# Chunked RWKV-7 and GLA scans: a chunk's tail issued inside the next chunk's inverse, and its small products cut to 64 columns

## The chip, the cores and the metric

The kernel runs on one core of a Trainium2 chip. The metric is device time in microseconds (us) of one execution; the kernel before takes 3583.4 us (median of 3 runs, 3581.79 to 3586.96). Engines are named as in the profile: PE is TensorE (matmul), PEld its weight loads, DVE VectorE, ACT ScalarE, POOL GpSimd, SP SyncE, which issues the DMAs.

## The reference: what is computed

One layer of a hybrid model on 2176 tokens (128 context, 2048 latent): a projection feeds three mixers (RG-LRU, RWKV-7, GLA), their outputs are projected back and added; then comes an expert-choice MoE. The change touches only the two matrix-state scans, each run forward and backward:

```python
# RWKV-7, 6 heads of 64, per token
sa = einsum('dbhij,dbhj->dbhi', S, -kk_t)
S  = S * w_t + sa[..., None] * (kk_t * a_t) + v_t[..., None] * k_t
o  = einsum('dbhij,dbhj->dbhi', S, r_t)
# GLA, 4 heads, keys 48, values 96, per chunk of 64 tokens
o = att @ v + (q * exp(b)) @ S
S = S * exp(b_last)[..., None] + (k * exp(b_last - b)).T @ v
```

## The kernel before, in words

The scans are one stage of the program, `stage_scans`, between the mixers' projection and the mixers' output. It takes 34 chunks of 64 tokens (`NCH`; 2 of context). The two directions are the two groups g = 0 and 1 and are worked on together. A group holds 3 tiles of 2 RWKV heads, one head in partitions 0 to 63 and one in 64 to 127 (`HALVES`), and 2 tiles of 2 GLA heads.

For RWKV a chunk needs the inverse of a triangular 64x64 matrix for each head. It is built by doubling, in five levels. A level l is `joined(c, l)` (PE: LM times T into the banks pY), `joined` on DVE (adds the identity, giving Ys), `grown(c, l)` (PE: Ys times U into the banks pYU), then `turned(c, l)` on DVE (transposes it into T) and `grown` on ACT (copies it to U). ACT's copy waits until DVE has transposed (`t_step`), except at level 5. A level's first product needs the T of the level before, so the levels are one chain through PE and DVE, and other products stand between them to cover it. These others are, in words: `values_seen` and `read_out` (keys against decayed keys and against reads, to KR and RK), `state_seen` (the state read by the chunk, to X), `keys_by_token` (BK, a transpose), `strict` (the next chunk's triangular matrix), `keys_turned`, and `attention` (GLA, 7 products for each tile and group).

What follows the inverse is here called the tail: `corrected` (U times X, written to SV), `state_grown` (the new RWKV state), `old_state_out` and `chunk_out` (the two parts of the output), `gla_added` and `gla_output` (the GLA state and output). The tail of chunk c has the banks pY, pYU and the free part of g1, and stands behind level 5 of chunk c; chunk c+1 begins when it is issued.

Each engine executes what it is given in order, and waits on semaphores; the order of each engine's work is written out by hand, in four functions `chunk(c)` (POOL, ACT, PE, DVE) and in SP's loop. So a wait holds up all that stands behind it on its engine. `SP` loads chunk c+3 after `freed(c)`, which waits for the states and outputs of chunk c, and then stores chunk c.

A product of `heads` is two matmuls, one for each half of the partitions, with 64 rows and 64 columns of the array each. `read_out` and `keys_by_token` use 64 rows and 128 columns, `state_grown` and `chunk_out` 128 rows and 64 columns. All are fp32, and the trace has two records for each such matmul: 12 matmuls of a level are 24 records.

## Time and profile before

| what | value |
|---|---|
| median of 3 runs | 3583.4 us |
| the profiled execution | 3593.6 us, its span 3591.9 us |
| PE busy in the span | 3171.3 us (88%) |
| DVE, ACT, POOL busy | 2275.4, 1611.8, 840.6 us |
| scans, first to last product | about 981 to 1825 us of the span |
| TensorE clock granted, mean of the span | 0.944 of full speed |

In a timeline row the first number is when the group of instructions starts, the second how long it lasts; x24 is the number of records; a bracket gives how long the engine was idle before it and what ended that. Records of PE overlap, and their ends are modelled: the time that a group really takes from the engine is the difference between its start and the next one's. A name such as scn_b is a PSUM bank with its number left out.

### The profile page before, as it was taken

The numbers are of one execution on the slowest core, as the hardware profiler recorded it, in microseconds if no ns is written. First come the engines' busy times: TensorE is split into PE (matmuls) and PEld (weight loads), VectorE is DVE, ScalarE is ACT, GpSimd is POOL, SyncE is SP. The second block draws the span as 40 slices with busy tenths as digits, with TensorE's granted clock in tenths as the row PEclk, the third lists the DMA queues.
The fourth block names the chain that finished last, engine by engine and source line by source line (L and its number), as shares of the span: only waits on it lengthen the run. The fifth ranks groups of instructions, "written<-read, shape, count | busy, mean of one in ns | idle before, by whom it ended". The sixth has DMA issues, their size and how long they took to land. (4 is left out here: it accounts for less than half of the span.)

```text
span 3591.9 us, 91692 instructions
## 1 busy us (share of the span) xinstructions
PE 3171.3 (88%) x37497; PEld 2899.1 (81%) x37497; DVE 2275.4 (63%) x4488; ACT 1611.8 (45%) x2909; POOL 840.6 (23%) x1189
## 2 busy tenths in 40 slices
PE   4899979999599999999959981799999999999992
PEld 1887867767499889999957760799999999999992
DVE  2575548995467777777768768455555555555553
ACT  1412756665444444444446640344444444444442
POOL 0200000000165655666622200111211111121000
PEclk7999989999799999999979985899999999999996
DMA  4464335665644544444356632556666655666646
GB/s 177 110 208 154 98 92 189 207 190 164 179 103 97 125 128 103 101 96 96 85 136 190 188 105 94 171 184 188 191 207 187 188 184 185 188 203 192 187 150 217
DMA packets 582979, 560.14 MB, mean 156 GB/s; under 512 B 211408, under 2 KB 527120, under 8 KB 581692
## 3 DMA queue, kind: packets, MB, share of 16 engines
q1 hardware_dynamic: 552496, 467.21, 43.8%
q0 software_dynamic: 30160, 88.35, 8.9%
q8 instruction: 236, 3.87, 0.5%
q14 instruction: 87, 0.71, 0.1%
HBM read 418.20 MB, written 137.23 MB: 155 GB/s over the span
## 5 line engine op out<-in xcount | busy, mean ns | idle before, releaser
L3253 DVE TENSOR_TENSOR exp_wlo<-exp_raw,exp_whi 128x2048 fp32r<-128x2048 f32 x192 | 439.9, 2292 | 361.8 <-ACT exp_whi L3208 354.2
L3208 ACT CAST exp_whi<-exp_raw 128x2048 fp32r<-128x2048 f32 x189 | 360.0, 1905 | 75.2 <-DMA exp_raw<-in_w_up 75.2
L986 PE MATMUL mix_acc<-proj_hThi,mix_wlo 128*128 128x448 f32 (+3 forms) x920 | 357.0, 388 | 14.0 <-DVE mix_wlo L1354 14.0
L986 PE MATMUL mix_acc<-proj_hTlo,mix_whi 128*128 128x448 f32 (+3 forms) x920 | 334.8, 364 | 0.0
L986 PE MATMUL mix_acc<-proj_hThi,mix_whi 128*128 128x448 f32 (+3 forms) x920 | 334.5, 364 | 0.0
L3137 PE MATMUL moe_o<-moe_hidhi,exp_wlo 128*128 128x272 f32 x1024 | 306.2, 299 | 0.0
L3137 PE MATMUL moe_g<-moe_xThi,exp_wlo 128*128 128x272 f32 x1024 | 299.7, 293 | 1.0 <-DVE moe_xTlo L3257 1.0
L3124 POOL DMA_INDIRECT y<-moe_yo,exp_sel x32 | 51.3, 1603 | 1051.3 <-DVE moe_yo L3267 1046.4
L3137 PE MATMUL moe_g<-moe_xThi,exp_whi 128*128 128x272 f32 x1024 | 296.9, 290 | 0.0
L3137 PE MATMUL moe_u<-moe_xThi,exp_wlo 128*128 128x272 f32 x1024 | 296.6, 290 | 0.0
L3137 PE MATMUL moe_o<-moe_hidhi,exp_whi 128*128 128x272 f32 x1024 | 296.6, 290 | 0.0
L3137 PE MATMUL moe_u<-moe_xThi,exp_whi 128*128 128x272 f32 x1024 | 296.4, 289 | 0.0
L3137 PE MATMUL moe_g<-moe_xTlo,exp_whi 128*128 128x272 f32 x1024 | 295.6, 289 | 0.0
L3137 PE MATMUL moe_u<-moe_xTlo,exp_whi 128*128 128x272 f32 x1024 | 295.0, 288 | 0.0
L3137 PE MATMUL moe_o<-moe_hidlo,exp_whi 128*128 128x272 f32 x1024 | 294.5, 288 | 0.0
L1941 ACT COPY scn_U<-scn_b 128x192 f32<-128x192 f32 x340 | 106.4, 318 | 280.1 <-DVE scn_T L2251 204.8
L957 POOL DMA_DIRECT2D proj<-mix_out x115 | 62.5, 544 | 715.7 <-ACT mix_out L1126 715.7
L986 PEld LDWEIGHTS mix_acc<-proj_hThi,mix_wlo 128*128 128x128 f32 (+1 forms) x920 | 172.2, 187 | 59.4 <-issue 42.5
L3137 PEld LDWEIGHTS moe_g<-moe_xThi,exp_wlo 128*128 128x128 f32 x1024 | 193.5, 189 | 2.0 <-DVE moe_xTlo L3257 1.4
L3137 PEld LDWEIGHTS moe_o<-moe_hidhi,exp_wlo 128*128 128x128 f32 x1024 | 192.9, 188 | 1.8
L3137 PEld LDWEIGHTS moe_g<-moe_xTlo,exp_whi 128*128 128x128 f32 x1024 | 193.8, 189 | 0.0
L3137 PEld LDWEIGHTS moe_g<-moe_xThi,exp_whi 128*128 128x128 f32 x1024 | 193.3, 189 | 0.0
(369 smaller groups left out, 8556.2 us busy)
## 6 DMA issues: line engine op xcount, KB each, us to landing
exp_raw<-in_w_gate SPq DMA_DIRECT2D x64, 1024.0 KB, 5.3
exp_raw<-in_w_up SPq DMA_DIRECT2D x64, 1024.0 KB, 5.2
exp_raw<-in_w_down SPq DMA_DIRECT2D x64, 1024.0 KB, 5.3
scn_plain<-rec SPq DMA_DIRECT2D x68, 384.0 KB, 3.6
rec<-mix_arena SPq DMA_DIRECT2D x24, 896.0 KB, 4.3
proj<-mix_out POOLq DMA_DIRECT2D x88, 224.0 KB, 2.3
scn_grc<-grec SPq DMA_DIRECT2D x136, 128.0 KB, 3.9
mix_arena<-in_w_ada SPq DMA_DIRECT2D x12, 1024.0 KB, 6.5
```

Of the source, the lines that this page charges most:

```text
L957: pool.dma_start(proj[c0:c0 + width, t0:t0 + tn], out[n % OUTS][0:width, 0:tn]).then_inc(out_stored[n % OUTS], 16)
L986: mm = pe.matmul(acc[n % ACCS][0:width, 0:tn], wt[:, k, 0:width], hT[hp][:, k, t0:t0 + tn], start=k == 0 and i == 0, stop=k == KD - 1 and ...
L1941: act.copy(Ui[c % 2][g][:, :, :], v3(pYU[g])).then_inc(u_step[g], 1)
L3124: pool.indirect_dma_start(out=y, out_offset=bass.IndirectOffsetOnAxis(ap=row(e, b, n), axis=0), in_=yo[0:n, b, :], in_offset=None, compute ...
L3137: mm = pe.matmul(ps[:, 0:N_SLOT], w[b][wp][:, k, tile * P:(tile + 1) * P], x[xp][:, k, :], start=k == 0 and i == 0, stop=k == KD - 1 and i ...
L3208: act.copy(w[k % RING][0][:, :, :], raw[k % RAW][:, :, :]).then_inc(hi_done[k % RING], 1)
L3253: dve.tensor_tensor(w[k % RING][1][:, :, :], raw[k % RAW][:, :, :], w[k % RING][0][:, :, :], ALU.subtract).then_inc(lo_done[k % RING], 1)
```

## The change

Every engine's `chunk` now gets two flags and does its own chunk's work and the tail of the chunk before in one pass; there are 35 passes, the first without a tail, the last with nothing else. `corrected` and the new RWKV state have a bank region of their own (beside GLA's outputs, in g2), the RWKV output another (beside GLA's states, in g1). The two parts of the RWKV output are accumulated in one place, so `old_state_out`, ACT's copy Old and DVE's addition go, and ACT copies the output. `read_out` and `keys_by_token` are cut into twice as many products of 64 rows and 64 columns, whose four kinds lie in the four quarters of the array; the halves of SV change places for one of the two heads, which makes one load of SV for each group into two. On POOL the large products of a chunk go ahead of the small ones. New waits go with it: GLA's output copies wait for the RWKV state (`s_done`), `read_out` and `strict` too, GLA's states wait for `o_done`.

On PE, where a tail stood between two chunks before (SV, BK, RK: the operands of the new state and of the output; S: the state; plain: the chunk's records; b0 to b7: the banks):

```order
L1996 MATMUL scn_b6<-scn_S11,scn_plain0 64x64 x6
L2101 MATMUL scn_b0<-scn_SV0,scn_BK0 64x64 x6
L2101 MATMUL scn_b1<-scn_SV0,scn_BK1 64x64 x6
L2116 MATMUL scn_b2<-scn_SV0,scn_RK0 64x64 x6
L2116 MATMUL scn_b3<-scn_SV0,scn_RK1 64x64 x6
L1996 MATMUL scn_b6<-scn_gv0,scn_kT1 64x96 x4
L1996 MATMUL scn_b7<-scn_gS11,scn_qe1 64x96 x2
L1996 MATMUL scn_b7<-scn_gv0,scn_att1 64x96 x2
```

all products of one shape stood together. Now group 1's part of the tail stands ahead of level 2's second product (U, Ys), with `read_out` (b4 and b5 from plain) right behind it:

```order
L2033 MATMUL scn_b7<-scn_gS11,scn_qe1 64x96 x2
L2033 MATMUL scn_b7<-scn_gv0,scn_att1 64x96 x2
L2033 MATMUL scn_b6<-scn_S11,scn_plain0 64x64 x2
L2151 MATMUL scn_b6<-scn_SV0,scn_RK1 64x64 x2
L2033 MATMUL scn_b6<-scn_S11,scn_plain0 64x64 x2
L2151 MATMUL scn_b6<-scn_SV0,scn_RK1 64x64 x2
L2033 MATMUL scn_b6<-scn_S11,scn_plain0 64x64 x2
L2151 MATMUL scn_b6<-scn_SV0,scn_RK1 64x64 x2
L2138 MATMUL scn_b7<-scn_SV0,scn_BK1 64x64 x6
L2033 MATMUL scn_b2<-scn_U00,scn_Ys0 64x64 x6
L2033 MATMUL scn_b3<-scn_U10,scn_Ys1 64x64 x6
L2077 MATMUL scn_b4<-scn_plain1 64x64 x2
```

The products with the state (64 rows) and with RK (128 rows) now alternate, three times for each group.

On DVE the tail's work stood in one piece behind the sums of the attention (S: RWKV state, O: output, gS: GLA state), ahead of the next chunk's first Ys:

```order
L2306 SCALAR_TENSOR_TENSOR scn_S01<-scn_b0,scn_total,scn_Sd0 128x64 x3
L2306 SCALAR_TENSOR_TENSOR scn_S11<-scn_b1,scn_total,scn_Sd1 128x64 x3
L2298 TENSOR_TENSOR scn_O00<-scn_b2,scn_Old0 128x192
L2298 TENSOR_TENSOR scn_O10<-scn_b3,scn_Old1 128x192
L2288 SCALAR_TENSOR_TENSOR scn_gS01<-scn_gS01,scn_F00,scn_b4 128x96 x2
L2288 SCALAR_TENSOR_TENSOR scn_gS11<-scn_gS11,scn_F10,scn_b6 128x96 x2
L2246 TENSOR_TENSOR scn_Ys0<-scn_b0,scn_con 128x192
L2246 TENSOR_TENSOR scn_Ys1<-scn_b1,scn_con 128x192
```

Now group 1's state and both GLA states stand between the Ys and the transposes of level 2, ahead of the transposes that level 3 and ACT's copies need:

```order
L2291 STREAM_TRANSPOSE scn_T10<-scn_b3 128x192
L2339 SCALAR_TENSOR_TENSOR scn_S01<-scn_b5,scn_total,scn_Sd0 128x64 x3
L2286 TENSOR_TENSOR scn_Ys0<-scn_b0,scn_con 128x192
L2286 TENSOR_TENSOR scn_Ys1<-scn_b1,scn_con 128x192
L2339 SCALAR_TENSOR_TENSOR scn_S11<-scn_b7,scn_total,scn_Sd1 128x64 x3
L2329 SCALAR_TENSOR_TENSOR scn_gS01<-scn_gS01,scn_F01,scn_b4 128x96 x2
L2329 SCALAR_TENSOR_TENSOR scn_gS11<-scn_gS11,scn_F11,scn_b6 128x96 x2
L2291 STREAM_TRANSPOSE scn_T00<-scn_b2 128x192
L2291 STREAM_TRANSPOSE scn_T10<-scn_b3 128x192
L2301 TENSOR_TENSOR scn_RK0<-scn_b4,scn_con 128x3x64
```

The additions that made O are gone, and T00 and T10 are queued behind S11, gS01 and gS11.

On ACT the tail of a chunk stood behind its level 5:

```order
L1972 COPY scn_SV2<-scn_b0 64x3x64
L1972 COPY scn_SV2<-scn_b2 64x3x64
L1972 COPY scn_SV2<-scn_b1 64x3x64
L1972 COPY scn_SV2<-scn_b3 64x3x64
L1977 COPY scn_Old0<-scn_b4 128x192
L1977 COPY scn_Old1<-scn_b6 128x192
L1982 COPY scn_gO00<-scn_b5 128x192
L1982 COPY scn_gO10<-scn_b7 128x192
L1941 COPY scn_U01<-scn_b2 128x192
L1941 COPY scn_U11<-scn_b3 128x192
```

Now the outputs O and gO stand between the copies U of the next chunk's levels 1, 2 and 3:

```order
L1953 COPY scn_U01<-scn_b2 128x192
L1953 COPY scn_U11<-scn_b3 128x192
L1980 COPY scn_O00<-scn_b4 128x192
L1980 COPY scn_O10<-scn_b6 128x192
L1953 COPY scn_U01<-scn_b2 128x192
L1953 COPY scn_U11<-scn_b3 128x192
L1988 COPY scn_gO00<-scn_b5 128x192
L1988 COPY scn_gO10<-scn_b7 128x192
```

gO00 and gO10 stand behind the copies U01 and U11 of level 2, which wait for DVE's transposes.

The core of the diff:

```diff
-        pSA, pS, pO = [[pY[g], pYU[g]] for g in range(G)], pY, pYU
...
-        pOld = [g1[g][:, HW:2 * HW] for g in range(G)]
+        pO = [g1[g][:, HW:2 * HW] for g in range(G)]
+        pSA = pS = [g2[g][:, HW:2 * HW] for g in range(G)]
...
-            for c in range(NCH):
-                chunk(c)
+
+            for c in range(NCH + 1):
+                chunk(c, c < NCH, c > 0)
...
-                        sp.dma_start(SV[u][HIGH, g, :, :, :].rearrange("t j h v -> t (j h v)"), v_rows[rows, :]).then_inc(rec_in[u], 16)
                         for h in range(2):
+                            sp.dma_start(SV[u][HALVES[1 - h], g, :, h, :], v_rows[rows, :].rearrange("t (j h v) -> h t j v", h=2, j=UN)[h]).then_inc(rec_in[u], 16)
...
+                def chunk_out(g, c):
+                    u = c % 2
+                    act.wait_ge(o_mm[g], c + 1)
+                    if c >= 2:
+                        act.wait_ge(o_out[g][u], 32 * (c // 2))
+                    act.copy(Os[g][u][:, :, :], v3(pO[g])).then_inc(o_done[g], 1)
+
+                def gla_out(g, c):
+                    u = c % 2
+                    act.wait_ge(go_mm[g], c + 1)
+                    act.wait_ge(s_done[g], c + 1)
+                    if c >= 2:
+                        act.wait_ge(go_out[g][u], 32 * (c // 2))
+                    act.copy(gOs[g][u][:, :, :], g2[g][:, 0:GN * GLA_DV].rearrange("p (j x) -> p j x", j=GN)).then_inc(go_done[g], 1)
+
...
+                def chunk(c, own, tail):
+                    more = c + 1 < NCH
+                    if tail:
+                        corrected(c - 1)
+                    if own:
+                        if c:
+                            decays(1, c)
+                        grown(c, 1)
+                    if tail:
+                        chunk_out(0, c - 1)
+                        chunk_out(1, c - 1)
+                    if own:
+                        grown(c, 2)
+                    if tail:
+                        gla_out(0, c - 1)
+                        gla_out(1, c - 1)
+                    if own:
+                        grown(c, 3)
+                        found(c)
+                        keys_by_token(c)
+                        keys_turned(0, c)
+                        keys_turned(1, c)
+                        if more:
+                            magnitudes(0, c + 1)
+                        grown(c, 4)
+                        if more:
+                            decays(0, c + 1)
+                        grown(c, 5)
+                        if more:
+                            magnitudes(1, c + 1)
...
                     pe.wait_ge(o_done[0], c)
+                    pe.wait_ge(s_done[0], c)
                     pe.wait_ge(go_done[0], c)
                     for x, j in units(g):
                         for h, p in enumerate(HALVES):
-                            mm = pe.matmul(cols(pRK[g][h], x, C), plain[u][p, j, 2 * C:4 * C], plain[u][p, j, C:2 * C], start=True, stop=True)
+                            for half, keys in ((HALVES[h], slice(2 * C, 3 * C)), (HALVES[1 - h], slice(3 * C, 4 * C))):
+                                mm = pe.matmul(cols(pRK[g][h], x, C)[half], plain[u][p, j, keys], plain[u][p, j, C:2 * C], start=True, stop=True)
...
-                def old_state_out(g, c):
+                def chunk_out(g, c):
+
                     u, S = c % NB, Ss[segment(c)]
+                    pe.wait_ge(rk_done[g], c + 1)
+                    pe.wait_ge(sa_done[g], c + 1)
                     pe.wait_ge(masked[g], c + 1)
                     for x, j in units(g):
-                        mm = heads(cols(pOld[g], x, C), plain[u][:, j, C:2 * C], S[g][:, x, :])
-                    mm.then_inc(old_mm[g], 1)
-
-                def chunk_out(g, c):
-                    u = c % NB
-                    pe.wait_ge(rk_done[g], c + 1)
-                    for x in range(UN):
+                        out = cols(pO[g], x, C)
+                        heads(out, plain[u][:, j, C:2 * C], S[g][:, x, :], stop=False)
                         for h, p in enumerate(HALVES):
-                            mm = pe.matmul(cols(pO[g], x, C)[p], RK[g][:, x, h, :], SV[u][:, g, x, h, :], start=True, stop=True)
+                            mm = pe.matmul(out[p], RK[g][:, x, h, :], SV[u][:, g, x, h, :], start=False, stop=True)
                     mm.then_inc(o_mm[g], 1)
...
+                def chunk(c, own, tail):
+                    if own:
+                        joined(c, 1)
+                    if tail:
+                        for g in range(G):
+                            gla_added(g, c - 1)
+                        for g in range(G):
+                            corrected(g, c - 1)
+                    if own:
+                        grown(c, 1)
+                    if tail:
+                        gla_output(0, c - 1)
+                        chunk_out(0, c - 1)
+                        state_grown(0, c - 1)
+                    if own:
+                        joined(c, 2)
+                    if tail:
+                        gla_output(1, c - 1)
+                        chunk_out(1, c - 1)
+                        state_grown(1, c - 1)
+                    if own:
+                        grown(c, 2)
+                        if c in (NCH_CTX - 1, NCH_CTX):
+                            states_turned(c)
+                        read_out(0, c)
+                        read_out(1, c)
+                        joined(c, 3)
+                        values_seen(c)
+                        if c + 1 < NCH:
+                            strict(c + 1)
+                        grown(c, 3)
+                        state_seen(c)
+                        keys_by_token(c)
+                        joined(c, 4)
+                        keys_turned(c)
+                        attention(0, c)
+                        grown(c, 4)
+                        attention(1, c)
+                        joined(c, 5)
+                        grown(c, 5)
...
+                def chunk(c, own, tail):
+                    if own:
+                        joined(c, 1)
+                    if tail:
+                        attention_summed(1, c - 1)
+                    if own:
+                        turned(c, 1)
+                    if tail:
+                        state_grown(0, c - 1)
+                    if own:
+                        joined(c, 2)
+                    if tail:
+                        state_grown(1, c - 1)
+                        gla_state(0, c - 1)
+                        gla_state(1, c - 1)
+                    if own:
+                        turned(c, 2)
...
```

## Rows read from the trace of the kernel before

**Rows 1.** The scans' whole stretch: busy microseconds (instructions) by engine, granted clock, DMA share, GB/s

```profile
981.00:1825.00 844.00, 797.70 (x22352) 762.00 (x22352) 634.50 (x1771) 392.42 (x1088) 509.90 (x816) 0.98 0.43 101
```

**Rows 2.** Timeline of PE, one chunk: start, duration, instruction, records, [idle before]

```profile
1401.12 0.87 PE L1996 MATMUL scn_b<-scn_T,scn_LM 64*64 64x64 f32 x24
...
1406.42 0.92 PE L1996 MATMUL scn_b<-scn_U,scn_Ys 64*64 64x64 f32 x24 [0.94 <-DVE scn_Ys L2246]
...
1410.31 0.90 PE L1996 MATMUL scn_b<-scn_U,scn_Ys 64*64 64x64 f32 x24
1411.36 0.93 PE L2092 MATMUL scn_b<-scn_X,scn_U 64*64 64x64 f32 x24 [0.15 <-ACT scn_U L1941]
...
1412.76 0.54 PE L1996 MATMUL scn_b<-scn_S,scn_plain 64*64 64x64 f32 x12
1413.23 0.92 PE L2101 MATMUL scn_b<-scn_SV,scn_BK 128*64 128x64 f32 x24
...
1414.78 0.55 PE L1996 MATMUL scn_b<-scn_gv,scn_kT 64*64 64x96 f32 x8
```

**Rows 3.** Timeline of PE, the next chunk's head, where four-quarter products will stand

```profile
1416.63 0.92 PE L1996 MATMUL scn_b<-scn_plain 64*64 64x64 f32 x24
1417.47 0.89 PE L2037 MATMUL scn_b<-scn_plain 64*128 64x64 f32 x12
...
1419.95 0.92 PE L1996 MATMUL scn_b<-scn_T,scn_LM 64*64 64x64 f32 x24
...
1422.10 0.87 PE L1996 MATMUL scn_b<-scn_U,scn_Ys 64*64 64x64 f32 x24
1422.89 1.56 PE L2048 MATMUL scn_b<-scn_con,scn_plain 64*128 64x64 f32 x24
...
1425.13 0.87 PE L1996 MATMUL scn_b<-scn_T,scn_LM 64*64 64x64 f32 x24
1425.83 0.34 PE L1996 MATMUL scn_b<-scn_con,scn_kh 64*64 64x64 f32 x6
```

**Rows 4.** Timeline of DVE, the same chunk

```profile
1407.70 0.32 DVE L2237 TENSOR_TENSOR scn_U<-scn_LM,scn_con 128x192 f32<-128x192 f32 x1
...
1408.35 0.65 DVE L2267 TENSOR_TENSOR scn_AM<-scn_b,scn_gcon 128x512 f32<-128x512 f32 x1
...
1411.25 0.68 DVE L2267 TENSOR_TENSOR scn_AM<-scn_b,scn_gcon 128x512 f32<-128x512 f32 x1
...
1412.43 0.56 DVE L2276 TENSOR_TENSOR scn_AM<-scn_AM 128x384 f32<-128x384 f32 x1
...
1413.85 1.24 DVE L2306 SCALAR_TENSOR_TENSOR scn_S<-scn_b,scn_total,scn_Sd 128x64 f32<-128x64 f32 x6
...
1415.54 1.04 DVE L2288 SCALAR_TENSOR_TENSOR scn_gS<-scn_gS,scn_F,scn_b 128x96 f32<-128x96 f32 x4
...
1418.90 0.73 DVE L2251 STREAM_TRANSPOSE scn_T<-scn_b 128x192 f32<-128x192 f32 x2 [0.69 <-PE scn_b L1996]
```

**Rows 5.** Timeline of ACT, the same chunk

```profile
1416.04 0.32 ACT L1982 COPY scn_gO<-scn_b 128x192 f32<-128x192 f32 x1 [2.16 <-PE scn_b L1996]
1419.32 0.67 ACT L1941 COPY scn_U<-scn_b 128x192 f32<-128x192 f32 x2 [2.96 <-DVE scn_T L2251]
```

**Rows 6.** Timeline of PE, the longer of two idle stretches of 2 us

```profile
1234.25 0.39 PE L1996 MATMUL scn_b<-scn_U,scn_Ys 64*64 64x64 f32 x7 [2.04 <-issue]
```

**Rows 7.** Timeline of PE, an idle stretch of the following stage

```profile
1922.27 0.47 PE L2583 MATMUL out_o<-out_wohi,out_mlo 128*128 128x512 f32 x1 [1.97 <-DVE out_y L2721]
```

**Rows 8.** Windows behind these two idle stretches, columns as in rows 1

```profile
1234.00:1240.00 6.00, 5.49 (x113) 5.20 (x114) 2.09 (x9) 2.07 (x8) 2.42 (x3) 0.72 0.05 9
1922.00:1928.00 6.00, 5.73 (x25) 4.78 (x26) 3.62 (x11) 4.58 (x10) 2.25 (x3) 1.00 0.78 192
```

**Rows 9.** Timeline of SP's issues: a chunk's first load, and its first store

```profile
1416.66 0.33 SPq L1795 DMA_DIRECT2D scn_plain<-rec  x1
...
1429.93 2.49 SPq L1810 DMA_DIRECT2D o_gla<-scn_gO  x4
```

More of the change, by code:

```diff
@@ L1709, in stage_scans @@
         RK, BK = ([st.sb(f"{x}{g}", [P, UN, 2, C]) for g in range(G)] for x in ("RK", "BK"))
-        Old = [st.sb(f"Old{g}", [P, UN, C]) for g in range(G)]
         Os = [[st.sb(f"O{g}{u}", [P, UN, C]) for u in range(2)] for g in range(G)]
@@ L1957, in chunk, with corrected @@
                         last.then_inc(bk_done[g], 1)
-                    if more:
-                        decays(0, c + 1)
-                    keys_turned(0, c)
-                    keys_turned(1, c)
-                    grown(c, 3)
-                    if more:
-                        magnitudes(1, c + 1)
-                    grown(c, 4)
-                    if more:
-                        decays(1, c + 1)
-                    grown(c, 5)
+                def corrected(c):
                     for g in range(G):
-                        act.wait_ge(sa_mm[g], n)
-                        for h in range(2):
-                            last = act.copy(SV[c % NB][LOW, g, :, h, :], v3(pSA[g][h][LOW, :]))
+                        act.wait_ge(sa_mm[g], c + 1)
+                        for h, p in enumerate(HALVES):
+                            last = act.copy(SV[c % NB][p, g, :, h, :], v3(pSA[g])[p])
@@ L1973, in chunk @@
                         last.then_inc(sa_done[g], 1)
-                    for g in range(G):
-                        act.wait_ge(old_mm[g], n)
-                        act.wait_ge(o_done[g], c)
-                        act.copy(Old[g][:, :, :], v3(pOld[g])).then_inc(old_done[g], 1)
-                    for g in range(G):
-                        act.wait_ge(go_mm[g], n)
-                        if c >= 2:
-                            act.wait_ge(go_out[g][u], 32 * (c // 2))
-                        act.copy(gOs[g][u][:, :, :], g2[g][:, 0:GN * GLA_DV].rearrange("p (j x) -> p j x", j=GN)).then_inc(go_done[g], 1)
+                def chunk_out(g, c):
[4 more added lines that the diff above has]
+                    act.copy(Os[g][u][:, :, :], v3(pO[g])).then_inc(o_done[g], 1)
@@ L2047, in keys_by_token @@
                             for h, p in enumerate(HALVES):
-                                mm = pe.matmul(cols(pBK[g][h], x, C), plain[u][p, j, 2 * C:4 * C], eye[p], start=True, stop=True)
+                                for half, keys in ((HALVES[h], slice(2 * C, 3 * C)), (HALVES[1 - h], slice(3 * C, 4 * C))):
+                                    mm = pe.matmul(cols(pBK[g][h], x, C)[half], plain[u][p, j, keys], eye[p], start=True, stop=True)
                     mm.then_inc(bk_mm, 1)
@@ L2089, in corrected @@
                     pe.wait_ge(u_step[g], NL * (c + 1))
+                    pe.wait_ge(masked[g], c + 1)
                     for x in range(UN):
-                        for h, p in enumerate(HALVES):
-                            mm = pe.matmul(cols(pSA[g][h], x, C)[LOW], Ui[c % 2][g][p, x, :], Xs[g][p, x, :], start=True, stop=True)
+                        mm = heads(cols(pSA[g], x, C), Ui[c % 2][g][:, x, :], Xs[g][:, x, :])
                     mm.then_inc(sa_mm[g], 1)
@@ new lines, in chunk @@
+                def chunk(c, own, tail):
[4 more added lines that the diff above has]
+                            gla_added(g, c - 1)
+                        for g in range(G):
+                            corrected(g, c - 1)
[31 more added lines that the diff above has]
+                        grown(c, 5)
@@ L2316, in states_turned, with chunk @@
                         dve.tensor_copy(SX[:, :, :], bank[6][:, 0:G * HW].rearrange("p (j t) -> p j t", j=G * UN)).then_inc(sx_out, 1)
[L2318 removed]
+                def chunk(c, own, tail):
                     more = c + 1 < NCH
[L2320 to L2351 removed]
@@ new lines, in chunk @@
+                    if own:
+                        turned(c, 2)
+                        if c in (NCH_CTX - 1, NCH_CTX):
+                            states_turned(c)
+                        read_out(0, c)
+                        read_out(1, c)
+                        joined(c, 3)
+                        values_seen(0, c)
+                        values_seen(1, c)
+                        turned(c, 3)
+                        if more:
+                            strict(0, c + 1)
+                        joined(c, 4)
+                        if more:
+                            strict(1, c + 1)
+                            pairs(0, c + 1)
+                        turned(c, 4)
+                        attention_masked(0, c)
+                        joined(c, 5)
+                        if more:
+                            pairs(1, c + 1)
+                        attention_masked(1, c)
+                        attention_summed(0, c)
```

129 lines of the change are left out of this document (27 added, 102 removed).

## The prediction

> **What bounds the kernel now.** I read four things: the busy time of each engine over the scans' stretch, PE's timeline over one chunk, DVE's and ACT's timelines beside it, and the granted clock behind PE's longest waits. The first shows that only PE can be the bound: 797.7 of 844.0 us busy, against 634.5 for DVE and 392.4 for ACT [rows 1]. PE's timeline repeats every 24.0 us: the same product of level 3 starts at 1401.12 and at 1425.13 [rows 2, 3]. In it PE waits for two things. One is level 4's Ys, with 0.94 us idle ahead of the row at 1406.42 (about 1.1 us of issue time, since the ends of records are modelled some 0.2 us behind their issue). The other is the last U ahead of the correction: 24 records from 1410.31 to 1411.36 take 1.05 us, where 24 records without a wait take 0.70 (1425.13 to 1425.83), so 0.35 [rows 2, 3]. About 1.45 us of a chunk are waits that another order could remove; the rest is PE's own work. Whatever the change does is multiplied by some 33 chunks.
>
> **The change, part by part, on PE's chain for one chunk.**
>
> 1. *Quarters instead of 128 columns.* From 1416.63 to 1419.95 stand two groups of 24 records and `read_out`'s two groups of 12: 3.32 us. Without the 24s at 0.70 each, 1.92 are left. From 1422.10 to 1425.13 stand a level's product, the 24 records of `keys_by_token` and the next `strict`: 3.03, less 1.40 leaves 1.63 [rows 3]. Together 3.55 us, the changes between the two shapes included. After it there are 96 records, and no change of shape; at 29 ns (0.70/24) they take 2.80. This gives back 0.75. The price of a quarter product isn't in the trace. The near rows are a record with other halves (29 ns) and the correction's, where both halves of the rows go to the same columns: from 1411.36 to 1412.76 its 24 records and 16 GLA records take 1.40, and the 16 are half as long again. If all four quarters ran at once it could be half of it, 15 ns: 1.40 more given back. If it were as dear as a 128-column record, 62 ns (24 records in 1.49 at 1422.89), it would cost 3.2 more; I take 29, since every 64x64 row has it.
>
> 2. *Alternating shapes in `chunk_out`.* Before, PE changes to 128 rows once: 12 + 48 records from 1412.76 to 1414.78 take 2.02, and 60 at 29 ns would take 1.75, so one way there and back costs at most 0.27, and the way there alone 0.12 (12 records in 0.47 instead of 0.35) [rows 2]. After, it changes six times there and back (three for each group; the last leads on to `state_grown`). I take 0.15 for each, since the 0.27 also holds 48 records that may be slower themselves: 0.90 - 0.27 = +0.63. The bounds are 0 for each (-0.27 in all) and 0.27 (+1.35).
>
> 3. *The old waits go.* -1.45: levels 4 and 5 now have DVE's tail work taken from between them, and the correction stands behind the next chunk's first product.
>
> 4. *What is late next.* I follow DVE from level 5's second Ys, at 0. Behind it stand U and T of the next chunk (0.65, 1407.70 to 1408.35), group 1's masked attention (1.18, 1411.25 to 1412.43), group 0's sums (1.42, to 1413.85) and the next chunk's Ys (0.35 for the first): masked at 1.83, Ys at 3.60 [rows 4]. PE starts level 5's U product at -0.3 and then issues 0.70 + 0.70 + 0.33, so it waits 0.4 for the mask at 1.43; two GLA and correction blocks later (0.33 + 0.70) it is at 2.86 and waits 0.7 for Ys; I take 0.5, because the two waits share what is uncertain. Level 5's own Ys costs 0.3, as no product covers it any more. That is 1.2 together.
>
> 5. *The long wait.* `read_out` now stands right behind level 2's U product, and waits for `go_done[0]`, ACT's copy of GLA's output. The chain to it starts at PE's last record of group 1's new state, which lands 0.22 after its issue: DVE's three operations on S (0.62, half of 1.24), four on gS (1.04), the two transposes (0.73), then ACT's two copies U (0.67, of which 0.1 lies beside the transposes) and gO (0.32): 3.5 us [rows 4, 5]. In that time PE has only level 2's U product, 0.70, the 0.1 of a shape change, and what is in flight. That leaves a wait of 2.4 to 2.7; I take 2.4. All of it is on the path: behind `read_out` on PE stand level 3 and everything else, and DVE waits for PE there. The wait exists whatever 1 and 2 cost, since it starts from PE's last record.
>
> Sum for a chunk: -0.75 + 0.63 - 1.45 + 1.2 + 2.4 = +2.0 us, so a period of 26.0. The first pass has no tail and the 35th has only one, so nothing is won at the ends: 33 x 2.0 = +67.
>
> 6. *The clock.* The wait has a second price. An idle stretch of 2.04 us ahead of 1234.25 was followed by a clock of 0.72 over the next 6 us, which is the lower level of 1.2 GHz for 3.4 of them; one of 1.97 us ahead of 1922.27 was not, with 1.00 after it [rows 6 to 8]. A wait of 2.4 us is longer than both. Where the clock falls, some 3.4 us of PE's work double in time, 1.7 us of extra, and part of that lies under other waits; I take 1.2, in half of the chunks: 17 x 1.2 = +20. The bounds are none (0) and every chunk at the full price (34 x 1.7 = +58).
>
> 7. *The rest.* SP issues 16 loads from 1416.66 to 1429.93 and then 8 stores [rows 9]; two more loads at the mean of 0.83 make it 14.9. `freed` comes about 12 us later in the program than before, so the loads are all issued about 1 us into the chunk after; their first user, `strict`, stands 15 us into that chunk. Hidden, with some 10 us in hand. POOL's reordering moves the large products ahead; POOL idles in this stage (509.9 of 844.0 busy [rows 1]) and PE needs them only at attention, 14 us later. Removing Old and the addition takes ACT and DVE work that PE didn't wait for: 0.
>
> Sum: +67 + 20 = +87. Against the profiled execution's own 3593.6 us it is 3681; that execution is 0.3% above the median, and the median is what will be compared, so 3583.4 + 87 = 3670.
>
> The Trainium skill bears on step 1 from two sides. "TensorEngine Tiling (Array Packing)", Key Properties, says that different tiles of the array can run their weight loads and matmuls in parallel; read strictly, that is the 15 ns of step 1, and a result of its own below. "TensorE: Matmul & The Clock Gate", in the section on 56 ns against 53.3, says that start-to-start never drops below about 25 ns however small a product is; by that the quarters would give back an estimated 0.4 more per chunk at best, for a time of about 3657. No run so far shows either one for four quarters.
>
> **The rivals.**
>
> *The wait without the clock* (0.26). The 2.4 us stay, but the clock stays up, as it did behind 1.97 us. +67: 3650.
>
> *Four quarters at once* (0.14). For it: nothing in a quarter product uses another's rows and columns. Against it: halves of rows and halves of columns both show about 29 ns, no less. Then -1.40 more for a chunk, 46 in all: +21 to +41 with the clock, 3604 to 3624.
>
> *The array hides more than I count* (0.09), the case on the other side. One mechanism: products in separate quarters overlap, and so do the changes of shape between short groups, because neighbours no longer need the same part of the array. Step 1 gives 0.75 + 1.40 and step 2 -0.27 instead of +0.63: the sum is 2.0 - 1.40 - 0.90 = -0.3, times 33 is -10: 3573. It decides from the point where the two together give 2.0 us more than I count; the 0.12 of the first change of shape speaks against it.
>
> *The new waits are covered* (0.04). If ACT's copies did not have to follow DVE's transposes, gO would come 1.3 us sooner and PE's wait would be 1.1: +24. For no change at all the others would have to go too. The code has this wait, so it is unlikely.
>
> *Dear changes of shape* (0.07). 0.27 for each and a fallen clock in most chunks: 33 x 2.7 + 40 = +129: 3712.
>
> **How the numbers follow.** Forecast with the fallen clock 0.40, at 3670; its own range is 3650 to 3700. The others stand above. 0.2% of this time is 7 us, about what a measurement can tell from no change. Faster by more is the fourth case's most part, 0.08; within it a part of the third, fourth and fifth, 0.05; slower 0.87. The range for 8 in 10 leaves out the case on the other side and the dearest: 3603 to 3712.
>
> **What would show it.** Right: in PE's timeline of after, an idle stretch of about 2.4 us ahead of the first product of `read_out`, ended by ACT's copy gO; a period of about 26 us; clocks of 0.5 behind some of these waits; 24 quarter records in 0.70 us; no idle ahead of level 4's U product. Wrong: quarter records at 15 ns (step 1), groups of state and RK products that run on at 29 ns without a gap (step 2), an idle stretch below 1 us ahead of `read_out` (step 5), or a clock of 1.00 through the stage (step 6).

## The result

| | before | after |
|---|---|---|
| median | 3582.6 us (4 runs, 3580.4 to 3587.0) | 3723.1 us (4 runs, 3710.5 to 3729.1) |
| ratio | | 1.0386, 95% interval [1.0357, 1.0415] |
| scans, to the last product | 1824 us of the span | 1958 us |

The change costs 140 us by the medians (131 by the two profiled executions), where 87 were forecast with a range up to 3712: the direction was right, the size wrong. All of it lies in the scans. ACT's copies gO, one pair for each chunk, start at 1021.43 and, 32 passes later, at 1937.51, so a pass takes 28.6 us in the mean. The same copies of before lie 24.5 apart; the single chunk that the prediction read has 24.0, and 26.0 were forecast. One of the four executions of e1 below took 13700 us, which nothing here explains; it is in that median, but not in the ratio.

The whole stage in windows of after, and one stretch of 4 us in it (start:end, length, then busy us and instructions of PE, PEld, DVE, ACT, POOL, granted clock, DMA share, GB/s):

```profile
981.00:1956.00 975.00, 824.82 (x23944) 763.66 (x23946) 632.63 (x1695) 404.47 (x1085) 507.39 (x816) 0.95 0.38 88
1421.50:1425.50 4.00, 4.00 (x92) 4.00 (x88) 2.30 (x8) 0.00 (x0) 2.53 (x8) 0.57 0.59 148
```

Against [rows 1], PE's idle time is 150 us instead of 46, and its busy time 27 us longer although the work is less. PE's timeline of after, one tail and what follows it:

```profile
1411.77 0.34 PE L2033 MATMUL scn_b<-scn_gS,scn_qe 64*64 64x96 f32 x4
...
1412.44 0.28 PE L2033 MATMUL scn_b<-scn_S,scn_plain 64*64 64x64 f32 x4
1412.65 0.34 PE L2151 MATMUL scn_b<-scn_SV,scn_RK 128*64 128x64 f32 x4
1412.91 0.33 PE L2033 MATMUL scn_b<-scn_S,scn_plain 64*64 64x64 f32 x4
1413.17 0.34 PE L2151 MATMUL scn_b<-scn_SV,scn_RK 128*64 128x64 f32 x4
...
1413.87 0.52 PE L2138 MATMUL scn_b<-scn_SV,scn_BK 128*64 128x64 f32 x12
...
1417.16 0.52 PE L2138 MATMUL scn_b<-scn_SV,scn_BK 128*64 128x64 f32 x12
1417.61 0.92 PE L2033 MATMUL scn_b<-scn_U,scn_Ys 64*64 64x64 f32 x24
1420.56 0.93 PE L2077 MATMUL scn_b<-scn_plain 64*64 64x64 f32 x48 [2.04 <-ACT scn_gO L1988]
1421.28 1.06 PE L2033 MATMUL scn_b<-scn_T,scn_LM 64*64 64x64 f32 x24
1422.07 2.84 PE L2033 MATMUL scn_b<-scn_plain 64*64 64x64 f32 x48
1424.63 1.21 PE L2033 MATMUL scn_b<-scn_U,scn_Ys 64*64 64x64 f32 x24
...
1429.87 0.50 PE L2033 MATMUL scn_b<-scn_con,scn_kh 64*64 64x64 f32 x9 [0.55 <-issue]
```

Four things are to be seen. The forecast wait is there: 2.95 us from start to start at 1417.61 where the group takes 0.70, ended by gO. `read_out`, 48 records in 0.72 us, runs at 15 ns a record: half of the 29 that step 1 took, and less, too, than the floor of 25 ns that is quoted beside it. Four records of a short group take 0.26 us where the shape changes around them, not the 0.12 of 29 ns each. And behind the long wait 48 plain records take 2.56 us instead of 1.40: the clock's mean from 1421.5 to 1425.5 is 0.57, the lower level of 1.2 GHz for nearly all of it.

DVE's and ACT's timelines of after show the chain to gO, in the order that step 5 forecast: S, gS, T, then U and gO.

```profile
1417.72 0.67 DVE L2339 SCALAR_TENSOR_TENSOR scn_S<-scn_b,scn_total,scn_Sd 128x64 f32<-128x64 f32 x3 [2.09 <-PE scn_b L2138]
1418.31 0.98 DVE L2329 SCALAR_TENSOR_TENSOR scn_gS<-scn_gS,scn_F,scn_b 128x96 f32<-128x96 f32 x4
1419.20 0.64 DVE L2291 STREAM_TRANSPOSE scn_T<-scn_b 128x192 f32<-128x192 f32 x2
```

```profile
1419.62 0.58 ACT L1953 COPY scn_U<-scn_b 128x192 f32<-128x192 f32 x2 [1.92 <-DVE scn_T L2291]
1420.09 0.55 ACT L1988 COPY scn_gO<-scn_b 128x192 f32<-128x192 f32 x2
```

PE's waits from 1000 to 1825 us (line, what ended them: us in all, times, longest), of after and then of before:

```profile
PE scn_b L2077 <- ACT scn_gO L1988: 55.8, 29, 2.0
PE scn_b L2033 <- issue: 37.3, 46, 2.5
PE scn_b L2033 <- DVE scn_Ys L2286: 10.1, 29, 0.4
PE scn_b L2033 <- DVE scn_T L2279: 10.0, 22, 1.2
PE scn_b L2033 <- DVE scn_AM L2310: 6.8, 29, 0.2
```

```profile
PE scn_b L1996 <- DVE scn_Ys L2246: 20.7, 28, 0.9
PE scn_b L1996 <- issue: 12.2, 16, 4.0
PE scn_b L2092 <- ACT scn_U L1941: 4.6, 30, 0.3
```

The same wait over the whole stage, in the list of those who waited for ACT's copy (us, times):

```profile
PE scn_b L2077: 63.9, 33
```

The `issue` line of both lists is what the prediction did not have: PE stands still, often in the middle of a group, with no engine to wait for. The experiments show what that is.

### The profile page after: what moved, and what is told of

The parts are those of the page before. It is cut to its first block and busy times, and to the rows that moved or that the text cites. A ratio compares the mean times of both kernels' runs of the same rounds, so it can differ in the third digit from the quotient of the medians.

```text
span 3723.0 us, 95088 instructions
## 1 busy us (share of the span) xinstructions
PE 3202.0 (86%) x39129; PEld 2904.9 (78%) x39129; DVE 2275.5 (61%) x4420; ACT 1624.8 (44%) x2909; POOL 837.9 (23%) x1189
## 3 DMA queue, kind: packets, MB, share of 16 engines
q1 hardware_dynamic: 575344, 467.22, 42.4%
## 5 line engine op out<-in xcount | busy, mean ns | idle before, releaser
L1885 POOL TENSOR_TENSOR scn_KF<-scn_grc,scn_F 128x768 f32<-128x768 f32 x68 | 123.1, 1810 | 443.7 <-ACT scn_F L1941 422.1
L2033 PE MATMUL scn_b<-scn_T,scn_LM 64*64 64x64 f32 x4080 | 175.3, 230 | 23.2 <-DVE scn_T L2279 15.3
```

The costliest lines, as they stand in the source:

```text
L1885: pool.tensor_tensor(KF[g][:, :, :, :], k.unsqueeze(1).to_broadcast([P, LEVELS, GN, C]), f[:, 0:LEVELS, :, :], ALU.mult).then_inc(kf_done[ ...
L2033: mm = pe.matmul(out[p], lhsT[p], rhs[p], start=start, stop=stop)
```

## The experiments

Each ran beside the kernel before on the same chip; its median was 3584.4 us for the first four, 3581.5 for the next four, 3582.9 and 3581.8 for the last two batches. Two numbers of the table are counted in the scans: "code" is PE's idle time in stretches above 0.15 us that end at `issue`, over the whole stage, and "low" the time at the lower clock, from 1000 us on. e6, e9, e12 and e15 leave out most of the loads and so compute later chunks from old data: they show time alone.

| kernel | median us | ratio to before, 95% interval | code us | low us |
|---|---|---|---|---|
| before | | | 12.7 | 10 |
| after | 3723.1 | 1.0386 [1.0357, 1.0415] | 42.4 | 75 |
| e1 quarters alone, in before | 3607.1 | 1.0067 [1.0040, 1.0093] | 91.0 | 31 |
| e2 after, no alternation | 3682.3 | 1.0268 [1.0243, 1.0292] | 48.7 | 72 |
| e3 after, gO copied first | 3653.7 | 1.0197 [1.0176, 1.0217] | 50.8 | 0 |
| e4 after, filler in the wait | 3717.0 | 1.0372 [1.0350, 1.0394] | 56.6 | 17 |
| e5 after, e2 and e3 | 3615.3 | 1.0094 [1.0073, 1.0115] | 55.9 | 10 |
| e6 e1, tiny loads | 3552.9 | 0.9918 [0.9901, 0.9934] | 43.8 | 7 |
| e7 e1, quarters of 128 columns | 3601.6 | 1.0056 [1.0037, 1.0074] | 59.4 | 17 |
| e8 before, keys_by_token in quarters | 3587.9 | 1.0020 [1.0009, 1.0030] | 42.6 | 14 |
| e9 before, tiny loads | 3574.8 | 0.9977 [0.9967, 0.9987] | 2.2 | 3 |
| e10 e1, loads spread | 3589.5 | 1.0019 [1.0007, 1.0031] | 76.2 | 14 |
| e11 e5, loads spread | 3599.7 | 1.0050 [1.0034, 1.0066] | 48.7 | 0 |
| e12 e7, tiny loads | 3554.2 | 0.9913 [0.9890, 0.9935] | 14.9 | 7 |
| e13 e8, loads spread | 3579.3 | 0.9990 [0.9981, 0.9999] | 31.9 | 24 |
| e14 e11, half of read_out at 128 columns | 3655.4 | 1.0210 [1.0186, 1.0234] | 22.4 | 61 |
| e15 after, tiny loads | 3687.9 | 1.0296 [1.0280, 1.0312] | 18.1 | 58 |

**e1, the quarters by themselves** (step 1).

```diff
-   mm = pe.matmul(cols(pRK[g][h], x, C), plain[u][p, j, 2 * C:4 * C], plain[u][p, j, C:2 * C], ...)
+   for half, keys in ((LOW, slice(2 * C, 3 * C)), (HIGH, slice(3 * C, 4 * C))):
+       mm = pe.matmul(cols(pRK[g][h], x, C)[half], plain[u][p, j, keys], plain[u][p, j, C:2 * C], ...)
(keys_by_token likewise)
```

> The kernel before with one part of the change alone: read_out and keys_by_token as products of 64 rows and 64 columns in the four quarters, order and waits as before. Theory A (a quarter record costs 17 ns, as the changed kernel's trace has it: 29.4 + 27.1 us for 3209 records, where the 128-column records took 53.8 + 50.2 us): about -47 us, 3536. Rival B (the gain comes back because PE now runs through its code faster and waits more often for it; the changed kernel has about 42 us of waits that no semaphore ends, the one before 12): -20 to -30, 3553 to 3563. Rival C (quarters at 29 ns, as I predicted, and something else made them look short): -25 at most with the changes of shape, 3558, and 29 ns in the trace.

Slower by 24 us by the ratio, not faster: every expectation missed. The quarters themselves are cheap (28.6 and 27.0 us for the two groups, 17 ns a record), yet PE waits 91 us at `issue` instead of 13. One such wait, in PE's timeline of e1, and then the DMA queues' packets, MB and share of 16 engines in the single microseconds 1525, 1526 and 1527 of it (q1 is data, q8 the instruction queue with blocks of 16 KB):

```profile
1526.03 0.86 PE L2050 MATMUL scn_b<-scn_con,scn_plain 64*64 64x64 f32 x42
...
1526.73 0.91 PE L1996 MATMUL scn_b<-scn_plain 64*64 64x64 f32 x23
1529.83 0.91 PE L1996 MATMUL scn_b<-scn_T,scn_LM 64*64 64x64 f32 x24 [2.19 <-issue]
```

```profile
q1 hardware_dynamic: 185, 0.12, 93.8%
...
q1 hardware_dynamic: 78, 0.24, 66.8%
...
q1 hardware_dynamic: 626, 0.23, 87.4%
q8 instruction: 1, 0.02, 5.8%
```

PE runs dry behind the quarters at about 1527.4, only then does a block of its instructions start to move (at 1527.49), and the next product starts 2.3 us later. All of these idle stretches look so: each of the 81 of e1 ends 2.2 to 3.2 us (median 2.5) after the start of such a block. The places where they end, counted in PE's records, settle what they are: those of all 81 stretches lie on one line, 125.15 records for each block, and none is off by more than 1.2; the 18 of before lie 124.95 apart and are off by 0.6 at most. PE stops where its instructions in hand run out. By this line PE still has 90 records ahead of it when a block starts in before (median; 57 to 114 for nine blocks in ten), and it begins some 66 in the next 2.45 us, so most blocks do no harm. In e1 the median is 77, but 40 of its 192 blocks start with 50 records or fewer in hand, against 3 of the 179 of before. The instruction queue of before from 1000 to 1825 us:

```profile
q8 instruction: 177, 2.90, 1.5%
```

In that time PE executed 22132 records, 125 for a block, and in no kernel did two blocks start less than 3.2 us apart.

The Trainium skill, "Runtime: NRT & Kernel Launch", Instruction fetch mechanics, has the 16 KiB blocks of 256 instructions, and says that crossing a boundary is mostly hidden. The blocks agree with the trace (250 for 125 records, if each record is a product and its weight load). Mostly hidden they are in before (12.7 us of waits), but not in e1 (91 us), and here the measurement decides.

**e2, no alternation** (step 2). All products with the state go ahead of those with RK.

```diff
                     for x, j in units(g):
-                        out = cols(pO[g], x, C)
-                        heads(out, plain[u][:, j, C:2 * C], S[g][:, x, :], stop=False)
+                        heads(cols(pO[g], x, C), plain[u][:, j, C:2 * C], S[g][:, x, :], start=x == 0, stop=False)
+                    for x in range(UN):
                         for h, p in enumerate(HALVES):
-                            mm = pe.matmul(out[p], RK[g][:, x, h, :], SV[u][:, g, x, h, :], start=False, stop=True)
+                            mm = pe.matmul(cols(pO[g], x, C)[p], RK[g][:, x, h, :], SV[u][:, g, x, h, :], start=False, stop=x == UN - 1)
```

> The changed kernel, but in chunk_out all three products with the state come first and then all six with RK, so PE changes shape there and back twice in a chunk instead of six times. Theory A (each way there and back costs 0.25 to 0.3 us, as four records of a group take 0.26 instead of 0.12): 4 x 0.27 x 33 = -35 us, 3688. Rival (short groups are slow because they accumulate into one place, or the time sits under other waits): within 8 us of 3723.

41 us faster than after, near the 35 expected. Its groups in PE's timeline, which took 0.26 us for each four records before the edit:

```profile
1424.58 0.51 PE L2033 MATMUL scn_b<-scn_S,scn_plain 64*64 64x64 f32 x12
1425.03 0.57 PE L2151 MATMUL scn_b<-scn_SV,scn_RK 128*64 128x64 f32 x12
1425.43 0.52 PE L2138 MATMUL scn_b<-scn_SV,scn_BK 128*64 128x64 f32 x12
```

12 and 12 records take 0.85 us from start to start; alternating, from 1412.44 to 1413.87, they took 1.43. So the six pieces instead of two cost 0.58 a group, 0.15 for each of the four changes that went. One change, not a way there and back, costs 0.15. The Trainium skill, "TensorEngine Tiling (Array Packing)", Key Properties, says that a change of tiling mode drains the engine; the 0.15 us of each change agrees.

**e3, gO copied first** (step 5). On ACT `gla_out(0, c - 1)` and `gla_out(1, c - 1)` go ahead of `grown(c, 2)`.

> The changed kernel, but ACT copies GLA's outputs ahead of its copies U of level 2, so read_out no longer waits for copies that wait for DVE's transposes. Theory A (this chain makes the 1.94 us of idle ahead of read_out): the wait falls to the 0.5 to 0.8 us that DVE's GLA state still needs, -1.3 x 33 = -43, and the clock falls more rarely, -15 to -30 more: 3650 to 3680. Rival (another wait takes its place, the transposes of level 2 ahead of level 3): the idle moves to level 3's first product and the time stays within 10 us of 3723.

69 us faster than after, as expected (3650 to 3680). PE's timeline at the same place, and the two largest waits of e3 that are not `issue`:

```profile
1413.28 0.91 PE L2033 MATMUL scn_b<-scn_U,scn_Ys 64*64 64x64 f32 x24
1414.57 0.93 PE L2077 MATMUL scn_b<-scn_plain 64*64 64x64 f32 x48 [0.37 <-DVE scn_gS L2329]
```

```profile
PE scn_b L2033 <- DVE scn_T L2279: 12.6, 21, 1.3
PE scn_b L2077 <- DVE scn_gS L2329: 10.8, 29, 0.4
```

The wait is 0.37 instead of 2.04, and from 1000 us on the clock never falls. One wait, caused by the place of two copies on ACT, was with the fallen clock behind it half of the change's whole loss.

**e4, filler in the wait** (step 6). Six useless products of 384 columns behind level 2's U.

```diff
+                        if tail:
+                            for _ in range(3):
+                                for p in HALVES:
+                                    pe.matmul(bank[0][p, 0:384], eye[p], gcon[p, 0:384], start=True, stop=True)
                         read_out(0, c)
```

> The changed kernel with six useless products of 384 columns (64 rows each, results never read, written over a region that level 3 overwrites) behind level 2's U product, about 1.9 us of PE work inside the wait ahead of read_out. It prices the clock alone. Theory A (the fallen clock costs 25 to 35 us: 75 us of the stage at half speed against 10 before): the clock stays up and the time falls by that, 3690 to 3700. Rival (the slow stretches lie under other waits): within 8 us of 3723, with the clock up. If the products stick out of the wait, up to +10 is to be added.

6 us faster; the expectation was missed, and the rival's time met. The fillers take 72 us in all and replace 64 us of the wait, the low clock falls from 75 to 17 us, which is worth half of the 58, 29 us, and waits for code grow by 14: 72 - 64 - 29 + 14 = -7. The sum closes, but it puts the 29 in by halving and doesn't measure it apart: that the clock's price in after is some 29 to 37 us is an estimate from the time at the lower clock, which e4 does not contradict.

**e5, e2 and e3 together.**

> The changed kernel with both earlier cures together: all products with the state ahead of those with RK, and ACT's copies of GLA's output ahead of its copies U of level 2. If the two are separate terms, they add: 3723 - 41 - 69 = 3613. If the waits for code (idle of PE in mid-group that ends with the arrival of its instructions) grow where other waits go, as they did where only the quarters were put in (12 to some 90 us), it is 3620 to 3640.

3615.3, where 3613 were expected of two separate terms: they add. 34 us of loss stay.

**e6, e7, e9 and e12: two causes of the waits for code.** Tiny loads cut the two largest kinds of a chunk's loads to one partition, with as many DMAs as before; e7 lets the quarters stream 128 columns instead of 64 (all but 272 of the 3264 records; `keys_by_token` goes through its tiles backwards for it).

```diff
                     u, at = c % NB, reached(c)
+                    few = slice(0, 1) if c >= NB else slice(0, P)
...
-                        sp.dma_start(plain[u][:, js, :]..., chunk_rec...)
+                        sp.dma_start(plain[u][few, js, :]..., chunk_rec[few]...)
```

(GLA's records likewise.)

> The kernel before with the quarters alone (3607.1, some 90 us of waits for code), and from the fourth chunk on each load of the chunk's records and of GLA's records moves one partition instead of 128, with as many DMAs and waits (the later chunks are then computed from old data). Theory of collisions: PE's instructions arrive late because they share the DMA engines with the chunk's loads; then the waits for code fall to about 12 us, and the time to 3607 - 80 = about 3530. Theory of the backlog: a fetch takes 2.4 us from its start whatever else is moved, and only the products that PE's queue already holds cover it; quarters at 15 to 19 ns drain it too soon. Then nothing changes: 3595 to 3610, 70 to 90 us of waits for code.

> The kernel before with the same number of quarter products as in the quarters alone, but each streams 128 columns instead of 64 (the results are the same, the surplus is written over), so that the instructions are as many and the array's work is about as long as with the 128-column shape. Theory of the backlog: what counts is how long the queued products keep the array busy; waits for code fall back to 12 to 30 us, time 3575 to 3600. Theory of the count: more instructions mean more fetches, each with its wait; the waits stay at 80 to 90 us and the time is 3584 + 75 = about 3660.

> The kernel before, with the loads of the chunk's records and of GLA's records from the fourth chunk on cut to one partition (old data are computed with). It is the control of the quarters with tiny loads, 3552.9. Theory of the shared engines: the fetch of PE's instructions is held back by loads, and only a full queue of slow products covers it; before has 12.7 us of waits for code, so at most 15 us are won here: 3566 to 3580, and the quarters, with loads out of the way, are a gain of 15 to 25 us. Rival: the loads cost time elsewhere (ports, other engines), the 54 us won with the quarters were mostly that, and this one comes out at 3530 to 3550.

> The kernel before with quarters that stream 128 columns (3601.6, 59 us of waits for code) and loads cut to one partition from the fourth chunk on. If the waits have two causes, a fetch held back by loads and a queue that short products drain, both are taken away here, and waits for code fall to 10 to 20 us, 3550 to 3570. If the number of instructions is a cause by itself, some 40 us of them stay, as in the 64-column quarters with tiny loads (44 us).

Waits for code, in us:

| | products of 128 columns (before) | quarters, 128 streamed | quarters, 64 streamed |
|---|---|---|---|
| all loads | 12.7 | 59.4 | 91.0 |
| tiny loads | 2.2 | 14.9 | 43.8 |

Neither rival of e6 was right alone: without the loads half of the 91 us goes. Neither was one of e7's: 59 us stayed, where one had 12 to 30 and the other 80 to 90. Both columns and rows of the table count, and e9 and e12 came out as the theory of two causes had them. The loads hold back the start of a block: in e1, the 67 blocks that started with the DMA engines over 50% busy in the next 2.4 us were followed by 1.13 us of wait in the mean, the 76 at 20 to 50% by 0.18, the 49 below that by 0.03. How long the block itself moves (1.0 to 1.1 us in the median) and how long after its start a waiting PE goes on (2.4 to 2.6) hardly differs between all these kernels. The delay lies ahead of the start: where the DMA engines were over 80% busy in the microsecond before it (53 blocks of e1), PE had 35 records left when the block started, where they were below 50% (119 blocks) 87, both in the median; and with tiny loads 8 blocks instead of 40 start with 50 records or fewer. No record shows when a block was asked for, so the place of the delay is read from these counts. The second cause is the queue: quarters in e7 take 28 to 31 ns a record, as long as any other product, and cover more than those of 16 to 19. With loads out of the way 29 of 44 us vanish by that alone. The number of instructions is also a cause: e7's array work is that of before (95 us against 104 in the two groups), but takes twice as many records there, and its waits are 47 us longer. e6 also shows that quarters are a gain once the loads are out of the way: 22 us faster than e9, though it waits 41 us more for code.

**e8, e10, e13, e11: fewer quarters, and loads spread.** In the last three, large and small loads and the stores alternate on SP, and the second direction's loads wait for level 3:

```diff
+                        if g and more:
+                            sp.wait_ge(y_mm[0], NL * (c + 1) + 3)
+                        (one large load, then a third of the small loads and stores, three times)
```

> The kernel before with only keys_by_token in quarters (24 more matmuls a chunk at most, in one place). Its 24 records at 50 us in all over the stage become 48 at 18.6 ns, 29 us: 20 us given back. If waits for code come in proportion to the quarter groups, half of those with both, +40: 3605. If read_out's quarters, which stand between other short waits, are what drains the queue, keys_by_token alone costs few: 3565 to 3580, faster than before.

> The kernel before with the quarters, and SP's issues in another order: large and small loads and the stores of the chunk before alternate, and the loads of the second direction wait for level 3 of the chunk. The same transfers, spread over the period. Theory of the shared engines: in the quarters alone a fetch that began with the DMA engines 50 to 80% busy was followed by a wait of 1.2 us in the mean, one with 20 to 50% by 0.2 us; with fewer of the first kind, waits for code fall from 91 to 45 to 70 us and the time from 3607 to 3560 to 3590. If the loads have no part in it: 3600 to 3612.

> The kernel before with keys_by_token alone in quarters (3587.9 against 3581.5; 43 us of waits for code) and SP's issues spread. By the shared engines, spreading took 18 us from the kernel with both groups in quarters, which had 91 us of such waits; with 43 it should take about 8: 3575 to 3583, no slower than before. No part of the loads: 3588.

> The changed kernel with its products in blocks, the copies of GLA's output first (together 3615), and SP's issues spread as in the quarters' run. It has 56 us of waits for code. Shared engines: 20 to 30 us of them go: 3585 to 3597, about as long as before. No part of the loads: 3610 to 3620.

e8 missed its gain by the waits for code (43 us). Spreading took 18 us from e1, 9 from e8, 16 from e5, but only 15, 11 and 7 us of their waits for code; in e10 45 to 70 us of these were expected and 76 stayed, and e11 fell 3 us short of the time expected. Of the kernels that compute everything e13 alone is not slower than before: 2.5 us faster, with an interval that barely leaves out 1. No version of the changed order got there: with all cures it is 17 us slower.

**e14, half of read_out back.** The three products of partitions 0 to 63 with 128 columns, then the others in quarters.

> The changed kernel with all cures (3599.7, 49 us of waits for code) and half of read_out's products back at 128 columns (those of partitions 0 to 63; 6 matmuls a chunk fewer in all, 12 records). Theory of the queue: fewer and longer products cover the fetches; waits for code fall by 5 to 15 us, the products cost 10 us more: 3595 to 3605, so no cure. If quarters were free of such a price, it is 3610.

It came out 56 us above e11, 50 above its range, by an error of my own design. PE's timeline, and the windows of this stretch and of the next:

```profile
1413.02 0.88 PE L2113 MATMUL scn_b<-scn_plain 64*128 64x64 f32 x6 [0.37 <-DVE scn_gS L2368]
1413.82 0.56 PE L2116 MATMUL scn_b<-scn_plain 64*64 64x64 f32 x12
```

```profile
1413.00:1415.50 2.50, 2.48 (x39) 2.28 (x41) 0.97 (x4) 0.58 (x2) 2.50 (x7) 0.99 0.39 74
1415.50:1419.00 3.50, 3.50 (x78) 3.50 (x71) 2.30 (x8) 0.00 (x0) 3.50 (x11) 0.52 0.54 147
```

Six records take 0.80 us, 133 ns each, twice the 62 to 70 ns that such a record took in before, where products of the lower and the upper partitions alternate: these neighbours in the same rows of the array don't overlap. All of `read_out` takes 86 us of the stage instead of 26 in e11, a part of it at the lower clock. The clock fell behind them although the wait ahead was 0.37 us only, so a long wait isn't the one thing that brings it down. e14 says nothing on what it was made for, except that waits for code did fall, to 22 us.

**e15, after with tiny loads.**

> The changed kernel as it is (3723.1; 42 us of waits for code, 75 us at the lower clock), with the loads of the records cut to one partition from the fourth chunk on. Shared engines: waits for code fall to 5 to 20 us as they did in the other three kernels with such loads, and 25 to 40 us are won: 3683 to 3698. Rival: here the long wait for ACT's copy sets the period, most of the code waits lie beside it, and less than 15 us are won: 3708 or more.

35 us faster, as expected, and waits for code fall by 24 us to 18; 17 us less are spent at the lower clock. The loads cost the changed kernel 35 us, the kernel before 8.

## Why the prediction was wrong

The direction came from step 5, and that was right. Term by term, over 33 chunks:

1. *Quarters*: forecast -25. The two groups fell from 104 us (53.8 and 50.2, start to start) to 56.5: -47. The assumed 29 ns was 15 to 19; the rival of four quarters at once had the mechanism right. This error made the forecast slower by 22 us, and so hid a part of the others: that the forecast came as near as it did owes something to luck.
2. *Alternation*: forecast +21. The groups of S, RK and BK rose from 106 to 154 us, +48, and undoing it won 41. The 0.27 of before, which I read as an upper bound of one way there and back, was the price itself, and more: a change costs 0.15 each way.
3. and 4. *Small waits*: forecast -48 and +40. The old ones (Ys and U, 25.3 us in 825) went; the new ones (Ys, T, mask) are 26.9 in the same stretch. Both signs and the small sum were right, both sizes too large: the one chunk that was read had 1.45 us of old waits, the mean of the stage is 0.75.
5. *The wait at read_out*: forecast +79, measured 64 (63.9 us in 33 waits, over the whole stage). Right in place, chain and nearly size; e3 confirms it.
6. *The clock*: forecast +20. 65 us more at half speed are at most +32, and with e4's sum some 30 fit. It fell behind 20 of 31 long waits, where I took half, and for 3.4 us each time; so the mechanism was right, and the size 10 us short.
7. *The rest*: forecast 0, "hidden, with some 10 us in hand". The loads are hidden for their data, but not for PE's instructions, which share the DMA engines: +30 of waits for code, and 27 us more of cost by loads than before (e15 and e9). This is the step that failed in kind; no rival had it. The idle stretches that ended at `issue` stood in the profile of before: [rows 6] is one, PE goes on there 2.4 us after the start of a block at 1231.83, and I read that row only for the clock behind it.

The terms, -47 + 48 + 64 + 30 + 30 = 125, are read from the profiled executions, which differ by 131. They overlap, since stretches at the lower clock are in the groups' times too, so that this nearness proves little, and the rest I can't place one by one. By experiment the sum closes: 41 (e2) and 69 (e3) leave 34, of which 16 go with the spreading of loads (e11). The last 17 may be the 36 us more of waits for code less what the quarters give; that was not shown, since e14, made for it, failed.

## What to carry over

Small products that run side by side in the array are cheap only as long as their instructions arrive: before cutting products, look for idle stretches of PE that end at `issue`, see whether they end at one spacing in records (here 125), and ask how many records PE can still run in the 2.5 us behind a block's start. Keep products of one shape together, alternate only between halves of the same shape, and never put a copy that frees a bank behind one that waits for another engine. Transfers that are hidden for their data can still delay the instructions.

## What the runs showed of the hardware

- Four quarter products at once: 15 to 19 ns a record with 64 columns streamed (after, e1), 28 to 31 ns with 128 (e7); a pair of 64x128 products in the two halves 62 to 70 (before); such products one behind the other in the same rows 133 (e14). So neighbours that lie in different parts of the array overlap almost wholly: twice 62 to 70 is the 133 of those that share their rows.
- A change of shape between 64 and 128 rows costs 0.15 us each time (after against e2: 1.43 and 0.85 us for the same 24 records, four changes apart).
- A block of PE's instructions is 16 KB and 125 records of these products. A waiting PE goes on about 2.5 us after the block's start (2.2 to 3.2 in e1), and blocks started no closer than 3.2 us in any run; in 125 records at 29 ns, 3.6 us, there is little to spare. Loads delay the start: waits for code fell from 91 to 44 us without them.
- The clock fell behind waits of some 2.0 us in 20 of 31 passes of after and in 17 of 31 of e15, never behind 0.37 us in e3, and in e14 behind 0.37 us and products that fill a half of the array.
